# Softmax attention of a hybrid decoder step: the row sums inverted as 128 by 2 and spread by a product, one head's turned scores copied by VectorE, a third buffer for mask rows, another queue order

## The chip, the cores and the metric

The kernel runs on one core of one Trainium2 chip. Its engines run side by side and meet through semaphores: TensorE (PE; its weight loads are shown apart as PEld), VectorE (DVE), ScalarE (ACT), GpSimd (POOL) and SyncE (SP), which here only issues transfers from HBM. The metric is the device time of one execution in microseconds.

## The reference

One inference step of a decoder trunk for 512 prompt tokens and 8 sample tokens (each with 256 past tokens) that share all weights. The first layer has dilated softmax attention (8 heads) beside gated linear attention, the second has sparse attention with an indexer that picks up to 128 keys per query (16 heads, 4 of keys and values). Each layer ends with a feed-forward part. What matters here is the softmax, which both layers share:

```python
def gathered_attention(q, kg, vg, bias, valid):
    ...
    s = jnp.einsum('btngd,btknd->btkng', qg, kg).reshape(bx, t, k, h).astype(jnp.float32) + bias
    s = jnp.where(valid[..., None], s, -jnp.inf)
    lse = jax.nn.logsumexp(s, axis=2)
    p = jnp.exp(s - lse[:, :, None, :]).reshape(bx, t, k, n_kv, grp)
    o = jnp.einsum('btkng,btknd->btngd', p.astype(vg.dtype), vg).reshape(bx, t, h, d)
    return o, lse
```

## The kernel before

The kernel is written engine by engine: each engine has its own program, in the order in which it is written, and waits on semaphores by hand. Most of the span is one long weight stream: SP loads weight blocks of 512 KB into `w_raw` (two places), ScalarE splits off their high part (L1115), GpSimd their low part (L451, `w_lo`), and TensorE multiplies (L567). SP's `weights(b0, b1)` waits before each load until the block of two loads earlier has been split (`w_lo`).

Between the projections stand the two attention stages. Instead of gathering keys, each computes dense causal scores and adds a mask that holds the position bias and what is left out.

- **Stage A** (first layer; 246 to 333.5 us of the span): 4 pairs of heads by 4 blocks of 128 queries, 16 units.
- **Stage C** (second layer; 1005.5 to 1161 us): 8 pairs by 4 blocks, 32 units.

A **unit** is one pair of heads and one block `qb` of queries; its width is W = 128 (qb + 1) keys: 128, 256, 384, 512, and again. The 512 queries of a pair lie in `q_hiC` and `q_loC` (high and low parts, split by GpSimd).

The loop `attention` is written once on each of TensorE, ScalarE and VectorE, and its iteration i works on several units at once:

- **TensorE**: `scores(i)` (L645, three products a head, waits `t_x` until the scores of unit i-1 have been read), `turn(i-1)` (L657, transposes of the exponentials, 128x128 each, in PSUM bank 2 + head; waits `t_e` and, for the bank, `t_c`), `out(i-2)` (L669, weights times values; waits `t_c` and `t_n`). Behind that, without a wait, the **sums product** (L674): the row sums in `stat` spread over 64 columns and multiplied with the identity, so that PSUM holds each query's sum once per output row, 128x128 in the second quarter of bank 4 + u % 2; it counts `t_v`.
- **ScalarE**: `exps(i)` (L1188, one exponential a head, its row sum into `stat`; waits `t_v` of unit i-2, since `stat` has two places, and `t_x`), then `copy(i-1)` (L1198, both heads from PSUM to `tmp` or `ptC`; waits `t_t`, counts `t_c`).
- **VectorE**: `add_bias(i)` (L1481, score plus mask, with the running row minimum into `stat`; waits `t_s`, in stage C also `C_bm`), then `normalise(i-3)`: reciprocal of the 128x128 sums in PSUM (L1490) and product with the unit's output (L1492), counted in `t_n`.
- **GpSimd**, in stage C: splits each pair's queries (L541, L543) and makes each unit's mask, `biasC` plus `score`, the indexer's cut (L551, counts `C_bm`).
- **SP**: `pair_biases` fetches a pair's mask rows from `scratch_rows` into `biasA` or `biasC`, two transfers of 256 KB a pair, one for each head. There are two places, so pair p waits until pair p-2 has been read.

On top of the loop lies the attention of the sample group (`between(i)`): in stage C its score products (`kcC`, L1029, iterations 3 to 6 and 12 to 15, one key cache each) and value products (`vcC`, L1042, iterations 20 to 23 and 27 to 30); its top-k on VectorE is a rank search with one step in each of iterations 2 to 10 (a maximum of eight, L1854, and a replacement). The key caches of sequences 4 to 7 take the places of the first four (`key pages`), and so do the values (`value pages`).

SP's queue ahead of and in stage C, in order: eight weight blocks with the indexer's pages; four weight blocks with key and value pages 0 to 3; six weight blocks; mask rows of pairs 0 and 1; key pages 4 to 7 (each waits until a place is free, `s_ks`); pairs 2 to 5; value pages 4 to 7 (`s_vs`); pairs 6 and 7; the weights after the attention. The indexer's products stand ahead of stage C, so that weight blocks that SP has issued before then wait for them.

## Time and profile before

| | before |
|---|---|
| device time, median of 3 runs | 1668.53 us (1666.94 to 1675.33) |
| the profiled execution | 1665.83 us, of which the span is 1664.0 us |
| PE busy | 1540.6 us (93%) |
| DVE busy | 726.3 us (44%) |
| ACT busy | 631.8 us (38%) |
| POOL busy | 653.2 us (39%) |
| mean granted TensorE clock | 0.95 |
| HBM | 139.11 MB read, 6.76 MB written |

### The profile page before, as it was taken

Reading aid. Unit: us, or ns where it says so; the run is one execution under the profiler, and the core shown is the slowest. Engines: PE = TensorE matmul, PEld = TensorE weight load, DVE = VectorE, ACT = ScalarE, POOL = GpSimd, SP = SyncE. Lnnn points to the kernel's source line nnn. Section 1 sums busy time; section 2 is a strip of 40 time slices with the busy share of each in tenths; the row PEclk is TensorE's granted clock in tenths of the full one; section 3 lists DMA queues with packets and bytes.
Section 4 is the critical chain, followed back from the end, with each engine's and each line's share of the span. In section 5 each row is a group of like instructions: output and inputs, shape, how many; then the busy total and the mean of one; then the engine's idle time right before and its main releaser. Section 6 shows DMA issues by size and latency. Waiting matters only on the chain.

```text
span 1664.0 us, 31509 instructions
## 1 busy us (share of the span) xinstructions
PE 1540.6 (93%) x12374; PEld 1451.0 (87%) x12374; DVE 726.3 (44%) x1119; ACT 631.8 (38%) x1050; POOL 653.2 (39%) x310
## 2 busy tenths in 40 slices
PE   3999989999999999999888997767999999999998
PEld 2999976799999999999887685545999999999998
DVE  5034225555545442213422766545555455422133
ACT  3242356434344333223533344334343433332224
POOL 2432250034444444443443145423344444444434
PEclk9999889899999999999988797788999999999999
DMA  3231143213223223332224022111223222333323
GB/s 128 87 107 64 63 177 103 83 63 102 88 92 97 88 88 102 101 98 92 66 93 134 26 67 70 41 44 39 76 90 97 92 88 88 90 99 101 100 82 123
DMA packets 53986, 146.88 MB, mean 88 GB/s; under 512 B 5485, under 2 KB 19593, under 8 KB 53402
## 3 DMA queue, kind: packets, MB, share of 16 engines
q1 hardware_dynamic: 52538, 139.27, 26.6%
q10 hardware_dynamic: 1376, 6.62, 1.1%
q8 instruction: 48, 0.79, 0.2%
q14 instruction: 24, 0.20, 0.0%
HBM read 139.11 MB, written 6.76 MB: 88 GB/s over the span
## 4 chain that ended last, share of the span: by engine, by line
PE 75%; issue 12%; DVE 4%; ACT 4%; POOL 3%; DMA 2%; SPq 1%; DVEq 0%; POOLq 0%; ACTq 0%
PE PS L567 63%; POOL w_lo L451 2%; DMA biasC<-scratch_rows 2%; PE PS L669 1%; PE PS L657 1%; PE PS L983 1%; PE PS L599 1%; PE PS L645 1%; PE PS L899 1%; PE PS L805 1%; PE PS L806 1%; DVE sqsum L1438 0%; DMA orow<-in_onehots 0%; ACT xC L1188 0%; DVE tmp L1564 0%
## 5 line engine op out<-in xcount | busy, mean ns | idle before, releaser
L451 POOL TENSOR_TENSOR w_lo<-w_raw,w_hi 128x1024 fp32r<-128x1024 f32 x217 | 533.2, 2458 | 868.2 <-ACT w_hi L1115 868.2
L1115 ACT ACTIVATE w_hi<-w_raw 128x1024 fp32r<-128x1024 f32 x217 | 229.8, 1060 | 764.8 <-PE PS L567 758.6
L567 PE MATMUL PS<-act,w_hi 128*128 128x260 f32 x2400 | 498.5, 289 | 20.9 <-POOL act L485 13.5
L567 PE MATMUL PS<-xg_hi,w_hi 128*128 128x260 f32 x1664 | 466.0, 283 | 4.0 <-POOL w_lo L451 4.0
L567 PE MATMUL PS<-xg_lo,w_hi 128*128 128x260 f32 x1664 | 465.4, 283 | 0.0
L567 PE MATMUL PS<-xg_hi,w_lo 128*128 128x260 f32 x1664 | 465.1, 283 | 0.0
L567 PEld LDWEIGHTS PS<-act,w_hi 128*128 128x128 f32 x2400 | 395.7, 194 | 30.6 <-issue 24.5
L567 PEld LDWEIGHTS PS<-xg_hi,w_hi 128*128 128x128 f32 x1664 | 311.6, 189 | 4.4 <-POOL w_lo L451 4.4
L567 PEld LDWEIGHTS PS<-xg_hi,w_lo 128*128 128x128 f32 x1664 | 311.9, 189 | 0.0
L567 PEld LDWEIGHTS PS<-xg_lo,w_hi 128*128 128x128 f32 x1664 | 311.9, 189 | 0.1
L567 PE MATMUL PS<-act,w_lo 128*128 128x260 f32 x944 | 267.9, 288 | 0.0
L567 PE MATMUL PS<-h_hi,w_lo 128*128 128x260 f32 x704 | 198.5, 282 | 0.0
L567 PE MATMUL PS<-h_hi,w_hi 128*128 128x260 f32 x704 | 198.3, 282 | 0.0
L567 PEld LDWEIGHTS PS<-act,w_lo 128*128 128x128 f32 x944 | 182.1, 195 | 0.0
L567 PEld LDWEIGHTS PS<-h_hi,w_hi 128*128 128x128 f32 x704 | 132.5, 188 | 0.0
L567 PEld LDWEIGHTS PS<-h_hi,w_lo 128*128 128x128 f32 x704 | 132.3, 188 | 0.0
L1550 DVE TENSOR_TENSOR x<-PS,x 128x520 f32 x16 | 11.2, 699 | 179.3 <-PE PS L567 179.3
L1538 DVE TENSOR_TENSOR act<-rs,h_hi 128x520 f32 x32 | 72.7, 2273 | 34.8 <-ACT h_hi L1238 34.8
L1532 DVE TENSOR_TENSOR tmp<-tmp,sq 128x520 f32<-128x520 f32 x44 | 59.9, 1361 | 64.2 <-ACT sq L1108 64.1
L1467 DVE SCALAR_TENSOR_TENSOR xg_lo<-x,vecs,xg_hi x32 | 71.9, 2246 | 34.8 <-ACT xg_hi L1140 34.8
L1188 ACT ACTIVATE xC<-xC,statC 128x128 f32<-128x128 f32 (+3 forms) x64 | 35.4, 554 | 87.0 <-PE PS L674 49.9
L1527 DVE TENSOR_TENSOR tmp<-PS,rs 128x520 f32<-128x520 f32 x44 | 30.8, 699 | 76.2 <-PE PS L567 75.2
(313 smaller groups left out, 1816.1 us busy)
## 6 DMA issues: line engine op xcount, KB each, us to landing
w_raw<-in_w SPq DMA_DIRECT2D x217, 512.0 KB, 3.5
biasC<-scratch_rows SPq DMA_DIRECT2D x16, 256.0 KB
yA<-in_cache_k SPq DMA_DIRECT2D x5, 512.0 KB, 6.3
x<-in_xT SPq DMA_DIRECT2D x4, 520.0 KB, 4.9
out_y<-x SPq DMA_DIRECT2D x8, 260.0 KB, 4.3
biasA<-scratch_rows SPq DMA_DIRECT2D x8, 256.0 KB
kcC<-in_pool_k SPq DMA_DIRECT2D x16, 128.0 KB, 2.5
vcC<-in_pool_v SPq DMA_DIRECT2D x16, 128.0 KB, 2.1
```

The source lines that it names most:

```text
L451: pool.tensor_tensor(w_lo[:, s, :], w_raw[:, s, :], w_hi[:, s, :].bitcast(F32), ALU.subtract).then_inc(S("w_lo"), 1)
L567: return pe.matmul(PS[:, 2 * place + half, 0:HALF], w[:, s, j * P:(j + 1) * P], r[:, c, HALF * half:HALF * half + HALF], start=first and n ...
L599: mm = pe.matmul(PS[:, bank + half, 0:HALF], weights, t[:, HALF * half:HALF * half + HALF], start=True, stop=True)
L645: mm = pe.matmul(PS[:, par, 0:W], q_of(pair, ql)[rows, qb * P:(qb + 1) * P], k_of(pair, kl)[rows, 0:W], start=n == 0, stop=n == 2)
L657: mm = pe.transpose(PS[:, 2 + par, cols], xs[:, u % 2, par, cols], ident)
L669: pe.matmul(PS[rows, bank, 0:P], v_of(pair, kb, par), pts[u % 2][:, par, kb * P:(kb + 1) * P], start=kb == 0, stop=kb == qb)
L1115: act.activation(w_hi[:, s, :], w_raw[:, s, :], ACT.Copy).then_inc(S("w_hi"), 1)
L1188: act.activation(xs[:, u % 2, par, 0:W], xs[:, u % 2, par, 0:W], ACT.Exp, bias=stat[:, u % 2, par, 0:1], scale=-1.0, accum_out=stat[:, u % ...
L1467: dve.scalar_tensor_tensor(xg_lo[:, one, :], x[:, one, :], vecs[:, bass.ds(m + gain, 1)], xg_hi[:, one, :].bitcast(F32), ALU.mult, ALU.sub ...
L1527: dve.tensor_tensor(halves(tmp[:, 0, :]), slot(0), halves(rs[:, 0, :]), ALU.mult).then_inc(S("free_v"), 1)
L1532: dve.tensor_tensor(tmp[:, 1, :], tmp[:, 1, :], sq[:, 0, :], ALU.mult).then_inc(S("f_s"), 1)
L1538: dve.tensor_tensor(lo, rs[:, 1:2, :], h_hi[:, bass.ds(f, 1), :].bitcast(F32), ALU.subtract).then_inc(S("h_lo"), 1)
```

## The change

**Loop.** The row sums are inverted where they stand, as 128 by 2 (`invert(i-1)` on VectorE), and it is the inverse that TensorE spreads by the same product. ScalarE copies the spread 128x128 from PSUM to `rr` (`spread(i-2)`), and VectorE's `normalise(i-3)` is only the product. The turned scores of the first head are copied by ScalarE (`t_c`), those of the second by VectorE (`t_d`). `stat` has four places instead of two, and the exponentials wait for the small reciprocal (`t_r`) of four units back. ScalarE's order is copy(i-1), exps(i), spread(i-2).

**Mask rows.** Stage C has three places: the two of `biasC`, and a part of `yC` that holds the indexer's queries before (free after `i_r` 24 and `d_z` 3). Stage A keeps two. In SP's queue pairs 0 and 1 stand ahead of the six weight blocks; then pairs 2 and 3, key pages 4 to 7, pairs 4 to 7, value pages 4 to 7.

**Names.** Semaphores of both stages are put together under common names (`smp_*`, `split_hi`, `split_lo`, `v_turned`, `v_ok`), with counts that go on.

```diff
...
-        statC = sb("statC", [P, 2, 2, 4], scope=sC)
+        statC = sb("statC", [P, 4, 2, 4], scope=sC)
...
+        biasC_place = (biasC[:, 0], biasC[:, 1], yC[:, 2:4, 0:SEQ])
...
-            def pair_biases(pairs, dst, rows, read, each):
+            def pair_biases(pairs, place, depth, rows, read, each):
...
-                    if p >= 2:
-                        sp.wait_ge(S(read), each * QB * (p - 1))
+                    if p >= depth:
+                        sp.wait_ge(S(read), each * QB * (p - depth + 1))
...
-                        sp.dma_start(dst[:, p % 2, par, :], src).then_inc(S(f"bias{p % 2}"), 16)
+                        sp.dma_start(place[p % depth][:, par, :], src).then_inc(S(f"bias{p % depth}"), 16)
...
+            def biases_c(*pairs):
+                pair_biases(pairs, biasC_place, 3, rows_c, "C_bm", 1)
+
             for b in range(4):
                 weights(B_C + 2 + NS + b, B_C + 3 + NS + b)
                 key_pages(b)
                 value_pages(b)
+            biases_c(0, 1)
             weights(B_C + 2 + NS + 4, B_OUT1 + 2)
-            rows_c = lambda p, par: 8 + 4 * (2 * (p // 4) + par) + p % 4
-            pair_biases(range(2), biasC, rows_c, "C_bm", 1)
+            sp.wait_ge(S("i_r"), 24)
+            sp.wait_ge(S("d_z"), 3)
+            biases_c(2, 3)
             for b in range(4, NS):
                 sp.wait_ge(S("s_ks"), NS + b - 3)
                 key_pages(b)
-            pair_biases(range(2, 6), biasC, rows_c, "C_bm", 1)
+            biases_c(4, 5, 6, 7)
             for b in range(4, NS):
                 sp.wait_ge(S("s_vs"), NS + b - 3)
                 value_pages(b)
-            pair_biases(range(6, 8), biasC, rows_c, "C_bm", 1)
...
-                            pe.wait_ge(S("t_c"), 2 * (first + u) + par - 1)
+                            pe.wait_ge(S("t_d" if par else "t_c"), first + u)
...
-                    pe.wait_ge(S("t_c"), 2 * (first + u + 1))
+                    pe.wait_ge(S("t_c"), first + u + 1)
+                    pe.wait_ge(S("t_d"), first + u + 1)
...
+                    pe.wait_ge(S("t_r"), first + u + 1)
                     for par in range(2):
-                        sums = stat[:, u % 2, par, 1:2].to_broadcast([P, HD])
-                        mm = pe.matmul(PS[HD * par:HD * par + HD, bank, P:2 * P], sums, ident,
+                        inverse = stat[:, u % 4, par, 2:3].to_broadcast([P, HD])
+                        mm = pe.matmul(PS[HD * par:HD * par + HD, bank, P:2 * P], inverse, ident,
                                        start=True, stop=True)
...
-                    if first + u > 1:
-                        act.wait_ge(S("t_v"), first + u - 1)
+                    if first + u > 3:
+                        act.wait_ge(S("t_r"), first + u - 3)
...
+                def spread(u):
+                    act.wait_ge(S("t_v"), first + u + 1)
+                    if first + u > 1:
+                        act.wait_ge(S("t_n"), first + u - 1)
+                    act.activation(rr[:, u % 2, :], PS[:, 4 + u % 2, P:2 * P], ACT.Copy).then_inc(S("t_rc"), 1)
...
+                    if 1 <= i <= count:
+                        copy(i - 1)
                     if i < count:
                         exps(i)
-                    if 1 <= i <= count:
-                        copy(i - 1)
+                    if 2 <= i < count + 2:
+                        spread(i - 2)
...
+                def copy(u):
+                    W = unit(u)[2]
+                    if first + u > 1:
+                        dve.wait_ge(S("t_v"), first + u - 1)
+                    dve.wait_ge(S("t_t"), 2 * (first + u) + 2)
+                    dve.tensor_copy(pts[u % 2][:, 1, 0:W], PS[:, 3, 0:W]).then_inc(S("t_d"), 1)
+
+                def invert(u):
+                    dve.wait_ge(S("t_e"), 2 * (first + u + 1))
+                    dve.reciprocal(stat[:, u % 4, :, 2:3], stat[:, u % 4, :, 1:2]).then_inc(S("t_r"), 1)
+
                 def normalise(u):
                     pair, qb, W = unit(u)
-                    bank = 4 + u % 2
-                    dve.wait_ge(S("t_v"), first + u + 1)
-                    if first + u > 1:
-                        dve.wait_ge(S("t_n"), first + u - 1)
-                    dve.reciprocal(rr[:, u % 2, :], PS[:, bank, P:2 * P]).then_inc(S("t_r"), 1)
-                    dve.wait_ge(S("t_r"), first + u + 1)
-                    dve.tensor_tensor(oraw[:, KC + pair, qb * P:(qb + 1) * P], PS[:, bank, 0:P],
+                    dve.wait_ge(S("t_rc"), first + u + 1)
+                    dve.tensor_tensor(oraw[:, KC + pair, qb * P:(qb + 1) * P], PS[:, 4 + u % 2, 0:P],
                                       rr[:, u % 2, :], ALU.mult).then_inc(S("t_n"), 1)
...
                     if i < count:
                         add_bias(i)
+                    if 1 <= i <= count:
+                        copy(i - 1)
+                        invert(i - 1)
                     if 3 <= i < count + 3:
                         normalise(i - 3)
...
```

What this does to the order of work stands best in three places.

ScalarE, inside stage C, two iterations (units 256 and 384 wide), before; `xC` holds the scores, and out<-in stands behind the line of the kernel, with the semaphores that the row waits on:

```order
L1188 ACTIVATE xC,statC<-xC,statC 128x256 [waits t_x,t_v]
L1188 ACTIVATE xC,statC<-xC,statC 128x256 [waits t_x]
L1198 ACTIVATE tmp<-PS 128x128 [waits t_t,t_v]
L1198 ACTIVATE tmp<-PS 128x128 [waits t_t]
L1188 ACTIVATE xC,statC<-xC,statC 128x384 [waits t_x,t_v]
L1188 ACTIVATE xC,statC<-xC,statC 128x384 [waits t_x]
L1198 ACTIVATE ptC<-PS 128x256 [waits t_t,t_v]
L1198 ACTIVATE ptC<-PS 128x256 [waits t_t]
L1202 ACTIVATE act<-oraw 128x512 [waits t_n]
```

The same stretch after the change:

```order
L1206 ACTIVATE tmp<-PS 128x128 [waits t_t,t_v]
L1197 ACTIVATE xC,statC<-xC,statC 128x256 [waits t_x,t_r]
L1197 ACTIVATE xC,statC<-xC,statC 128x256 [waits t_x]
L1212 ACTIVATE workC<-PS 128x128 [waits t_n,t_v]
L1206 ACTIVATE ptC<-PS 128x256 [waits t_t,t_v]
L1197 ACTIVATE xC,statC<-xC,statC 128x384 [waits t_x,t_r]
L1197 ACTIVATE xC,statC<-xC,statC 128x384 [waits t_x]
L1212 ACTIVATE workC<-PS 128x128 [waits t_n,t_v]
L1216 ACTIVATE act<-oraw 128x512 [waits t_n]
```

The copy of the unit before now stands ahead of the exponentials, only the first head's is left, and each iteration ends with the copy of the spread inverse (`workC` is where `rr` lies in stage C).

VectorE, one iteration of stage C, before (`ISA` is the sum of score and mask with its row minimum; the second `ISA` row moves that minimum into `statC`):

```order
L1481 ISA xC,statC<-PS,rs 128x256 [waits t_s,C_bm,t_t]
L1481 ISA statC 128x1
L1481 ISA xC,statC<-PS,rs 128x256 [waits t_s]
L1481 ISA statC 128x1
L1490 RECIPROCAL workC<-PS 128x128 [waits t_n,t_v]
L1492 TENSOR_TENSOR oraw<-PS,workC 128x128 [waits t_r]
```

and after:

```order
L1497 ISA xC,statC<-PS,rs 128x256 [waits t_s,C_bm,t_t]
L1497 ISA statC 128x1
L1497 ISA xC,statC<-PS,rs 128x256 [waits t_s]
L1497 ISA statC 128x1
L1505 COPY tmp<-PS 128x128 [waits t_t,t_v]
L1509 RECIPROCAL statC<-statC 128x2 [waits t_e]
L1514 TENSOR_TENSOR oraw<-PS,workC 128x128 [waits t_rc]
```

The copy of the second head and the small reciprocal stand between the mask sums and the product of the unit three back; the 128x128 reciprocal is gone.

SP's queue from the last value pages of sequence 3 to the first key page of sequence 4 (the branch rows are the loop over weight blocks; `TENSOR_LOAD ptab` reads a page's number), before:

```order
L420 DMA vcC<-in_pool_v 128x256
L331 UNCONDITIONAL_BRANCH
L331 ISA
L328 ISA [waits w_lo]
L328 DMA w_raw<-in_w 128x1024
...
L331 REGISTER_ALU
L331 COMPARE_AND_BRANCH
L348 DMA biasC<-scratch_rows 128x1x512 x4
L404 TENSOR_LOAD ptab [waits s_ks]
```

and after:

```order
L421 DMA vcC<-in_pool_v 128x256
L349 DMA biasC<-scratch_rows 128x1x512 x4
L332 UNCONDITIONAL_BRANCH
...
L329 ISA [waits w_lo]
L329 DMA w_raw<-in_w 128x1024
...
L349 DMA yC<-scratch_rows 128x1x512 [waits d_z,i_r]
L349 DMA yC<-scratch_rows 128x1x512
L349 DMA biasC<-scratch_rows 128x1x512 [waits C_bm]
L349 DMA biasC<-scratch_rows 128x1x512
L405 TENSOR_LOAD ptab [waits s_ks]
```

Pairs 0 and 1 (four transfers, `x4`) moved from behind the six weight blocks to ahead of them, and pairs 2 and 3 now stand between the blocks and the key pages, pair 2 with a wait for the third place.

## Rows read from the trace of the kernel before

**Rows 1.** Stages: stretch, length, busy (x) PE to POOL, clock, DMA share, GB/s.
```profile
246.00:333.50 87.50, 81.59 (x626) 60.08 (x626) 49.80 (x132) 43.09 (x124) 6.66 (x7) 0.89 0.32 99
1005.50:1161.00 155.50, 111.91 (x910) 83.78 (x910) 90.53 (x263) 64.39 (x204) 60.53 (x45) 0.81 0.13 43
1050.00:1055.00 5.00, 4.58 (x29) 3.31 (x30) 4.17 (x15) 1.96 (x8) 3.99 (x3) 0.50 0.13 50
1085.00:1090.00 5.00, 4.01 (x34) 2.67 (x34) 3.81 (x9) 3.75 (x13) 2.99 (x4) 1.00 0.02 5
```

**Rows 2.** Chain that ended last: start, us, what; two longest waits.
```profile
1034.42 12.88 DMA biasC<-scratch_rows
...
1111.32 12.87 DMA biasC<-scratch_rows
```

**Rows 3.** TensorE's timeline: start, us, line, out<-in [idle before <-what ended it].
```profile
1033.60 0.43 PE L645 MATMUL PS<-act,q_hiC 64*128 64x128 f32 x2
...
1048.66 0.81 PE L645 MATMUL PS<-act,q_hiC 64*128 64x256 f32 x3 [9.37 <-DVE statC L1481]
...
1108.44 0.45 PE L645 MATMUL PS<-k_C,q_hiC 64*128 64x128 f32 x4
...
1125.55 0.81 PE L645 MATMUL PS<-k_C,q_hiC 64*128 64x256 f32 x3 [13.27 <-DVE statC L1481]
...
1132.94 0.79 PE L645 MATMUL PS<-k_C,q_hiC 64*128 64x512 f32 x4
```

**Rows 4.** TensorE's timeline between those two waits.
```profile
1068.40 0.52 PE L645 MATMUL PS<-act,q_hiC 64*128 64x256 f32 x4
...
1077.12 1.14 PE L1029 MATMUL PS<-kcC,qzC 128*128 128x257 f32 x4
...
1078.19 0.45 PE L645 MATMUL PS<-k_C,q_hiC 64*128 64x128 f32 x4
...
1079.28 1.06 PE L657 MATMUL PS<-const,xC 128*128 128x128 f32 x8 [0.53 <-ACT tmp L1198]
...
1081.30 0.51 PE L645 MATMUL PS<-k_C,q_hiC 64*128 64x256 f32 x4
```

**Rows 5.** Waits of 1005 to 1161: engine, tile, line <- releaser: us, times, longest.
```profile
ACT xC L1188 <- PE PS L674: 49.9, 27, 4.0
```

**Rows 6.** TensorE's groups by shape, 1005.5 to 1161: busy, mean ns | idle before.
```profile
L657 PE MATMUL PS<-const,xC 128*128 128x128 f32 x160 | 30.0, 321 | 11.4 <-ACT tmp L1198 7.8 <-ACT ptC L1198 3.6
```

**Rows 7.** GpSimd's timeline, first mask sum of pair 3.
```profile
1057.92 0.73 POOL L551 TENSOR_TENSOR sq<-biasC,score 128x256 f32<-128x256 f32 x1 [1.64 <-DMA biasC<-scratch_rows]
```

**Rows 8.** SP's issues, 905 to 960.
```profile
909.46 1.44 SPq L420 DMA_DIRECT2D vcC<-in_pool_v  x2
944.59 14.65 SPq L328 DMA_DIRECT2D w_raw<-in_w  x3
```

**Rows 9.** DMA issues, 1110 to 1125: times, KB, median us from issue to landing.
```profile
w_raw<-in_w SPq DMA_DIRECT2D x1, 512.0 KB, 15.7
```

**Rows 10.** DMA issues of the whole span (page, part 6).
```profile
w_raw<-in_w SPq DMA_DIRECT2D x217, 512.0 KB, 3.5
```

**Rows 11.** ScalarE's groups by line and shape, 1004 to 1160.
```profile
L1198 ACT ACTIVATE tmp<-PS 128x128 f32<-128x128 f32 x16 | 3.4, 258 | 0.0
```

**Rows 12.** VectorE's groups by line and shape, 1004 to 1160.
```profile
L1490 DVE RECIPROCAL workC<-PS 128x128 f32<-128x128 f32 x32 | 30.5, 952 | 1.2 <-PE PS L674 1.2
...
L1854 DVE MAX8 mx<-wk 8x8 f32<-8x257 f32 x7 | 2.8, 406 | 0.0
...
L1832 DVE COPY vtokC<-PS 128x512 f32<-128x512 f32 x2 | 1.3, 676 | 0.0
...
L1587 DVE RECIPROCAL sstC<-sstC 128x1 f32<-128x1 f32 x1 | 0.2, 152 | 0.0
```

**Rows 13.** TensorE's weight loads, timeline, 1021 to 1024.
```profile
1022.43 0.63 PEld L669 LDWEIGHTS PS<-tmp,vtokC 128*64 128x64 f32 x12 [0.17 <-issue]
1023.03 0.25 PEld L674 LDWEIGHTS PS<-const,statC 128*64 128x64 f32 x4
```

More of the change, by code:

```diff
@@ L550, in _ @@
                 mask = score[:, qb, 0:W].unsqueeze(1).to_broadcast([P, 2, W])
-                pool.tensor_tensor(bmC[u % 2][:, :, 0:W], biasC[:, pair % 2, :, SEQ - W:SEQ], mask,
+                pool.tensor_tensor(bmC[u % 2][:, :, 0:W], biasC_place[pair % 3][:, :, SEQ - W:SEQ], mask,
                                    ALU.add).then_inc(S("C_bm"), 1)
@@ L882, in _ @@
             mm.then_inc(S("s_o"), 1)
-            pe.wait_ge(S("A_v"), QB)
+            pe.wait_ge(S("v_ok"), QB)
             pe.wait_ge(S("b_o"), 1)
             def ready_a(pair):
-                pe.wait_ge(S("A_st"), (1, 2, 5, 6)[pair])
+                pe.wait_ge(S("split_lo"), (1, 2, 5, 6)[pair])
                 pe.wait_ge(S("k_split"), 1)
@@ L1009, in _ @@
                 if kb % 2:
-                    mm.then_inc(S("C_vt"), 1)
+                    mm.then_inc(S("v_turned"), 1)
             sample_index(8)
-            pe.wait_ge(S("C_vtc"), 2)
+            pe.wait_ge(S("v_ok"), 6)
             def ready_c(pair):
-                pe.wait_ge(S("C_st"), pair + 1)
+                pe.wait_ge(S("split_lo"), 6 + pair + 1)
                 pe.wait_ge(S("k_split"), 3)
@@ L1178, in products_in, with attention @@
                     head_rms(q, q % 2)
-            def attention(first, count, xs, pts, stat, between):
+            def attention(first, count, xs, pts, stat, rr, between):
                 def exps(u):
                     W = unit(u)[2]
-                    if first + u > 1:
-                        act.wait_ge(S("t_v"), first + u - 1)
+                    if first + u > 3:
+                        act.wait_ge(S("t_r"), first + u - 3)
                     for par in range(2):
@@ L1195, in copy @@
                         act.wait_ge(S("t_v"), first + u - 1)
-                    for par in range(2):
-                        act.wait_ge(S("t_t"), 2 * (first + u) + par + 1)
-                        act.activation(pts[u % 2][:, par, 0:W], PS[:, 2 + par, 0:W], ACT.Copy).then_inc(S("t_c"), 1)
+                    act.wait_ge(S("t_t"), 2 * (first + u) + 1)
+                    act.activation(pts[u % 2][:, 0, 0:W], PS[:, 2, 0:W], ACT.Copy).then_inc(S("t_c"), 1)
+                def spread(u):
[3 more added lines that the diff above has]
+                    act.activation(rr[:, u % 2, :], PS[:, 4 + u % 2, P:2 * P], ACT.Copy).then_inc(S("t_rc"), 1)
                 def high_out(pair):
@@ L1469, in gained_lo, with attention @@
                                          ALU.subtract).then_inc(S("xg_lo"), 1)
-            def attention(first, count, xs, stat, rr, bias, between):
+            def attention(first, count, xs, pts, stat, rr, bias, between):
                 def add_bias(u):
@@ L1710, in _ @@
                 dst = qz[rows, 32 * r:32 * r + 31 * 65 + 1:65].rearrange("p (t b) -> p t b", t=4)
[L1711 removed]
+                dve.tensor_copy(dst, yA[rows, Y_Q:Y_Q + 4, SEQ:NT]).then_inc(S("smp_q"), 1)
             def new_key_a(b):
```

146 lines of the change are left out of this document (73 added, 73 removed).

## The prediction

> **What bounds the kernel now.** I read the busy shares first (table above): TensorE is busy 93% of the span, so time comes off only where TensorE stands still or runs at its lower clock. The view by stages shows where: in stage A it is busy 81.59 of 87.50 us at a mean granted clock of 0.89, in stage C 111.91 of 155.50 us at 0.81 [rows 1]. Everything that the diff touches lies in these two stages. The chain that ended last then shows two waits on a transfer of mask rows in stage C, 12.88 us at 1034.42 and 12.87 us at 1111.32 [rows 2]; no other transfer of that length stands on it there. TensorE's own timeline gives the price: scores of iteration 8 start at 1033.60 and those of iteration 9 at 1048.66; iteration 24 starts at 1108.44 and iteration 25 at 1125.55 [rows 3]. After each stall the clock is down (0.50 in 1050 to 1055, against 1.00 in 1085 to 1090 [rows 1]).
>
> The measure for an undisturbed iteration is 1068.40 to 1081.30: four iterations (scores 256, 384, 512 and 128 wide) take 12.90 us, three of them with a product for the sample group, 1.07 us from its start to the next product's [rows 4]. Less these 3.2 us that is 9.7 us for four, 2.4 us each, and only 0.53 us of it is a wait for ScalarE. So where sample products fill the gaps TensorE is nearly the bound already. The loop that the diff rewires (ScalarE's exponentials wait for the sums product of two units back: 49.9 us of ScalarE idle [rows 5]) costs TensorE far less than that idle time suggests: all waits before the turning products in stage C are 11.4 us [rows 6].
>
> **The change, part by part.**
>
> Third buffer and queue order. With two buffers the rows of pair p may be fetched only once pair p-2 has been read, one pair ahead, which at the pace above is 9.7 us. The transfer takes 12.9 us [rows 2], or 10.6 us when the next follows on its heels: pair 2 landed at 1034.42 + 12.88 = 1047.30, pair 3 released GpSimd at 1057.92 after a wait [rows 7]. 9.7 is less than 10.6, so two buffers are late even with prompt issue, and these two were not issued promptly: pair 2 stood on SP behind the key pages, pair 6 behind the value pages. Three buffers give two pairs of lead, 19.4 us, against 12.9; and pairs 2 and 6 now stand ahead of the pages that held them. I take both stalls as gone: 15.06 - 2.58 = 12.5 us and 17.11 - 2.58 = 14.5 us, where 2.58 is the iteration of the same shape, 1078.19 to 1081.30 less its wait of 0.53 [rows 3, 4]. **-27.0 us.**
>
> The slow clock behind the stalls goes with them. From 1048.66 to 1068.40 four iterations with one sample product took 19.74 us, 18.7 without it, against 9.7; I take 8.5 of these 9.0 because there is a second, small sample product in it. From 1125.55 to 1132.94 two took 7.4 against 4.9 [rows 3, 4]. **-11.0 us.** Lower bound 0, if TensorE finds no other work to keep its clock.
>
> What moves past what: pairs 0 and 1 now go out right after the value pages issued at 909.46, ahead of six weight loads, of which the first goes out at 944.59 [rows 8]. A weight load that stood behind mask rows took 15.7 us to land [rows 9], others 3.5 [rows 10]. Four transfers at 10.6 us a pair are through by about 911 + 21 = 932, so the indexer's products, which hold the next load back until 944.59, cover them with 12 us to spare; without that cover the first load would be up to 21 us late. Cost 0.
>
> ScalarE's and VectorE's part of the loop. Exponentials of unit u no longer wait for the sums product of u-2, and the copies of the two turned heads run on two engines at once. ScalarE gives up one copy per unit (258 ns or more) and gets the spreading copy of 128x128 from PSUM, for which the same-sized row gives 258 ns [rows 11]: nothing or less. VectorE loses the 128x128 reciprocal, 952 ns, and gets a reciprocal of 128x2 (152 ns for 128x1; at most the old 952) and a copy of one head, at most 676 ns for 512 columns [rows 12]. By the nearest rows that is -0.12 us at the widest unit; if the small reciprocal cost as much as the big one, +0.68. I take the first, as time per instruction here follows the columns. What this frees on TensorE is bounded by 0 and the 11.4 us of rows 6; part of those lie in the stretches already counted, and the start and the end keep theirs: **-6 us**. In stage A, where TensorE idles 5.9 us [rows 1], I take **-3**, between 0 and 5.9: its sample products cover half the stage already.
>
> Costs. VectorE carries one step of the sample group's rank search in each of nine iterations; its maximum alone takes 406 ns [rows 12], and the step has a second instruction over the same 257 columns, so some 0.9 us by estimate. Four of these iterations have a sample product on TensorE beside them, the other five do not, so VectorE could set the pace there: 0 to 4.5 us, I take **+2.3**. TensorE gets a new wait (for the small reciprocal) in the middle of what ran without a break: weight loads behind a wait show 0.17 us of issue time, those of the sums product, which had none, show nothing [rows 13]. 48 units by 0.17 is 8.2 us at most, and where TensorE waits anyway it costs nothing: **+6**. Behind a waiting sums product stand the next scores; the reciprocal that it waits for is issued an iteration earlier, so the wait itself should be empty.
>
> GpSimd's mask sums, renamed semaphores and the four-deep statistics change no work: 0.
>
> **Sum.** -27.0 - 11.0 - 6 - 3 + 2.3 + 6 = -38.7 us. On the profiled execution's own 1665.83 us that is 1627.1. The median of the runs stands 2.7 above it (1668.53), so I predict **1630 us**.
>
> **Rivals.**
>
> (1) A second bound takes the loop's place. VectorE (90.53 us busy in stage C [rows 1]) now holds a copy that waits for TensorE between the mask sum of one unit and that of the next, and ScalarE's copy stands ahead of the exponentials. If that in-order coupling costs what the old one cost, nothing of the 6 and 3 us comes, and the costs come in full (4.5 + 8.2): -27 - 11 + 12.7 = -25.3, 1643 us. For it: VectorE is the busier of the two. Against: every engine's sum per unit falls. Chance 0.16.
>
> (2) Mask rows or pages late again. If one of the two stalls stays (pair 6 or 7, because the faster loop asks sooner), 17 us of the gain are lost: 1647 us. For it: a pair's transfer (10.6 to 12.9 us) is no shorter than the new pace of a pair. Against: the 19.4 us of lead. The value pages 4 to 7 now go out behind pair 7; they are issued after iteration 20 and used in 27, seven iterations or about 17 us, against the 12.9 us that the rows ahead of them can last. Chance 0.08 for both. The Trainium skill, DMA: Bandwidth & Descriptors, section "Queues, rings and completion order", says that each DMA engine takes one queue's descriptors in ring order; by that rule those pages, which share SP's queue, wait for pair 7's rows, and would cost up to 12.9 us if the lead were used up. The trace agrees: 15.7 us for the load behind mask rows [rows 9], 3.5 for others [rows 10].
>
> (3) Slower than before: the clock. The new loop puts more, shorter waits between TensorE's products. Were the granted clock to stay at 0.50 (1.2 GHz) through stage C, eight rounds of 18.7 us and 16 sample products at twice 1.07 us would make 184 us, against 155.5 now: 1697 us. It decides from about two thirds of the stage's work on: at full clock the same work is 8 x 9.7 + 17 = 95 us, and (155.5 - 95) / (184 - 95) = 0.68. Against: in 1085 to 1090 the clock is 1.00 with TensorE busy 4.01 of 5 us [rows 1]. Chance 0.03.
>
> (4) Everything goes, the costs are nothing: -27 - 11 - 11.4 - 5.9 = -55.3, 1613 us. Chance 0.05.
>
> **How the numbers follow.** My forecast has 0.68. The range reaches from (4) to (2), 1612 to 1647, and leaves out (3) and a little on either side. A measurement of this kernel tells about 0.5% (8 us) from no change; only (3), and both stalls staying, fall outside "faster": faster 0.94, same 0.03, slower 0.03.
>
> **What would show it.** Right: no mask transfer on the chain within stage C; TensorE's scores start without a gap of more than 4 us after iteration 4; granted clock of stage C above 0.9; stage C some 115 to 120 us from first scores to the output projection instead of 155.5; stage A 84 to 87 us. The first weight load after the indexer lands in about 3.5 us. Wrong: a wait of GpSimd on mask rows (then rival 2), VectorE without idle time in stage C and TensorE waiting for its copies or row sums (rival 1), a clock under 0.8 there (rival 3). The step I trust least is the cost of the added wait on TensorE, which no row shows at that place.

## The result and the profile after

The changed kernel takes 1625.6 us (median of 4, 1623.1 to 1631.1) beside 1671.7 us for the kernel before, a ratio of 0.973 with an interval of 0.970 to 0.976. Timed once more beside the last experiments it took 1631.0 us (1619.4 to 1637.6), 0.977 of before (0.973 to 0.981). The forecast was 1630 us in 1612 to 1647.

| | after |
|---|---|
| the profiled execution | 1623.13 us, of which the span is 1621.3 us |
| PE busy | 1531.9 us (94%) |
| DVE / ACT / POOL busy | 708.2 / 628.8 / 652.4 us |
| mean granted TensorE clock | 0.961 |

Nearly all of the difference lies in stage C. The view by stages, with the columns of [rows 1], from the first score product of each attention stage to the first product of the output projection:

```profile
1004.74:1121.10 116.36, 103.22 (x910) 77.80 (x911) 80.55 (x294) 62.77 (x204) 60.81 (x45) 0.91 0.16 51
244.16:330.76 86.60, 84.20 (x627) 63.03 (x627) 42.13 (x148) 41.83 (x124) 6.54 (x7) 0.85 0.32 100
```

Stage C is now 116.4 us at a clock of 0.91; before it ran from 1005.57 to 1161.28, 155.7 us, at 0.81. Stage A is 86.6 us; before it ran from 246.10 to 333.54, 87.4 us. The spans differ by 42.7 us: 39.4 from stage C, 0.8 from stage A, and 2.5 from the rest of the execution.

TensorE's timeline, where the two stalls stood in [rows 3]: first scores of the stage, scores of iterations 8, 9, 24, 25 and 31.

```profile
1004.74 0.69 PE L652 MATMUL PS<-act,q_hiC 64*128 64x128 f32 x4 [1.47 <-DVE vtokC L1857]
...
1034.13 0.54 PE L652 MATMUL PS<-act,q_hiC 64*128 64x128 f32 x4
...
1037.58 0.61 PE L652 MATMUL PS<-act,q_hiC 64*128 64x256 f32 x3 [0.67 <-DVE statC L1497]
...
1089.09 0.44 PE L652 MATMUL PS<-k_C,q_hiC 64*128 64x128 f32 x4
...
1092.21 0.52 PE L652 MATMUL PS<-k_C,q_hiC 64*128 64x256 f32 x4
...
1109.64 0.74 PE L652 MATMUL PS<-k_C,q_hiC 64*128 64x512 f32 x4
```

Iterations 8 and 24 take 3.45 and 3.12 us, where they took 15.06 and 17.11. From first to last scores the stage takes 1109.64 - 1004.74 = 104.9 us, and 142.4 before (1005.57 to 1148.00). That stretch is the measure of the experiments below, since the rest of an execution disturbs it less than it does the time. The granted clock in the stage's first iterations still differs from execution to execution (table of experiment 9).

The groups by line and shape of stage C show the loop's terms (busy us, mean ns of one, idle before and what ended it): the turning products and the spreading product on TensorE, the copy and the small reciprocal on VectorE, ScalarE's spreading copy.

```profile
L664 PE MATMUL PS<-const,xC 128*128 128x128 f32 x160 | 27.1, 303 | 0.4 <-ACT xC L1197 0.3
...
L683 PE MATMUL PS<-const,statC 128*64 128x128 f32 x128 | 13.1, 285 | 0.0
...
L1505 DVE COPY ptC<-PS 128x512 f32<-128x512 f32 x8 | 5.5, 689 | 2.9 <-PE PS L664 2.9
...
L1509 DVE RECIPROCAL statC<-statC 128x2 f32<-128x2 f32 x32 | 5.0, 157 | 0.0
...
L1212 ACT ACTIVATE workC<-PS 128x128 f32<-128x128 f32 x32 | 8.4, 261 | 3.9 <-PE PS L683 2.7 <-DVE oraw L1514 1.1
```

The turning products waited 11.4 us in [rows 6] and wait 0.4 now; the spreading product, which has the new wait, never stood idle ahead. The single prices are as read: 157 ns for the small reciprocal, 689 for a copy of 512 columns, 261 for the spreading copy.

### The profile page after: what moved, and what is told of

Same layout as the page of the kernel before. It is cut to its first block, busy times and chain, and to the rows that moved or that the text cites. A ratio compares the mean times of both kernels' runs of the same rounds, so it can differ in the third digit from the quotient of the medians.

```text
span 1621.3 us, 31604 instructions
## 1 busy us (share of the span) xinstructions
PE 1531.9 (94%) x12374; PEld 1446.1 (89%) x12374; DVE 708.2 (44%) x1167; ACT 628.8 (39%) x1050; POOL 652.4 (40%) x310
## 4 chain that ended last, share of the span: by engine, by line
PE 76%; issue 12%; DVE 5%; ACT 3%; POOL 3%; DMA 0%; SPq 0%; DVEq 0%; POOLq 0%; ACTq 0%
PE PS L574 65%; POOL w_lo L458 2%; PE PS L652 2%; PE PS L992 1%; PE PS L606 1%; PE PS L664 1%; PE PS L677 1%; PE PS L908 1%; PE PS L1038 1%; DVE sqsum L1454 0%; PE PS L814 0%; PE PS L815 0%; DMA orow<-in_onehots 0%; DVE tmp L1589 0%; ACT tmp L1115 0%
## 5 line engine op out<-in xcount | busy, mean ns | idle before, releaser
L574 PE MATMUL PS<-act,w_hi 128*128 128x260 f32 x2400 | 497.8, 289 | 19.3 <-POOL act L492 12.7
L1575 DVE TENSOR_TENSOR x<-PS,x 128x520 f32 x16 | 11.2, 700 | 179.3 <-PE PS L574 179.3
L1552 DVE TENSOR_TENSOR tmp<-PS,rs 128x520 f32<-128x520 f32 x44 | 30.8, 700 | 75.8 <-PE PS L574 75.1
L1561 DVE TENSOR_TENSOR rs<-PS,tmp 128x520 f32<-128x520 f32 x44 | 30.8, 700 | 59.1 <-PE PS L574 58.9
```

The lines of the kernel that those rows point to most:

```text
L574: return pe.matmul(PS[:, 2 * place + half, 0:HALF], w[:, s, j * P:(j + 1) * P], r[:, c, HALF * half:HALF * half + HALF], start=first and n ...
L1552: dve.tensor_tensor(halves(tmp[:, 0, :]), slot(0), halves(rs[:, 0, :]), ALU.mult).then_inc(S("free_v"), 1)
L1561: dve.tensor_tensor(halves(rs[:, 1, :]), slot(1), halves(tmp[:, 1, :]), ALU.mult).then_inc(S("free_v"), 1)
```

## The experiments

The theory that the forecast rests on: the late mask rows carry the gain, by third place and queue order together, and the loop gives and costs about the same. The rivals: one of third place and order does it alone; or the loop carries a part of its own, by VectorE's reciprocal, by the two copies, or by ScalarE's order.

**1. The rows alone.** The loop of before, with three places and the new queue order:

```diff
-            pair_biases(range(2), biasC, rows_c, "C_bm", 1)
...
+            biases_c(0, 1)
             weights(B_C + 2 + NS + 4, B_OUT1 + 2)
+            sp.wait_ge(S("i_r"), 24)
+            sp.wait_ge(S("d_z"), 3)
+            biases_c(2, 3)
```

> The loop of before, with the third place and the new queue order alone. Theory (the mask rows carry the gain: both stalls and the slow clock behind them): about 36 of the 42 us come, time 1634 us (1629 to 1640) where before is 1671, stage C 118 to 122 us from its first scores to the output projection, no scores later than 4 us after iteration 8 or 24. Rival (the old loop, in which ScalarE's exponentials wait for the sums product, is the next bound as soon as the stalls are gone): 1645 us or more, iterations at 3.2 us or longer in the middle of the stage.

Measured: 1643.5 us, 0.982 of before (0.977 to 0.987); 112.2 us from first to last scores (1013.95 to 1126.12), 30.3 less than before. No scores came late by a stall (iteration 8 took 5.65 us, 24 took 3.76), but 7.3 us are left to the changed kernel. The profiled executions differ by more, spans of 1643.6 and 1621.3 us: 10.6 in stage C up to the output projection, 6.9 in stage A. ScalarE's wait from 1030 us on, in the columns of [rows 5]:

```profile
ACT xC L1195 <- PE PS L681: 45.4, 27, 4.0
```

And the turning products' group, first to last scores, in the columns of [rows 6]:

```profile
L664 PE MATMUL PS<-const,xC 128*128 128x128 f32 x146 | 25.2, 300 | 12.5 <-ACT tmp L1205 6.8 <-ACT ptC L1205 5.7
```

ScalarE's wait for the sums product is nearly as long as in [rows 5], and what TensorE pays for it as in [rows 6], 12.5 us. Both expectations are half right: the rows carry most, and the old loop is the next bound. The time lies between the two ranges (up to 1640, from 1645).

**2. The loop alone.** After the change, with two places and the old queue order:

```diff
-                pair_biases(pairs, biasC_place, 3, rows_c, "C_bm", 1)
+                pair_biases(pairs, biasC_place, 2, rows_c, "C_bm", 1)
...
-            biases_c(0, 1)
             weights(B_C + 2 + NS + 4, B_OUT1 + 2)
+            biases_c(0, 1)
...
-            biases_c(4, 5, 6, 7)
+            biases_c(2, 3, 4, 5)
...
+            biases_c(6, 7)
```

> The loop after the change, with two places and the queue order of before. Theory (the stalls are set by when the transfer is issued and how long it takes, not by the loop): both stalls stay, a little longer since the loop asks earlier; the gain is that of stage A and of the iterations between the stalls, 2 to 6 us: 1665 to 1669 us where before is 1671. Rival (the loop carries half of the gain): 1650 us or less.

Measured: 1653.9 us, 0.990 of before (0.988 to 0.992), 17 us faster, outside of what the theory allowed and short of the rival's 1650. In its profile the stalls stand as before (iterations 8 and 24 take 14.89 and 17.81 us), and first to last scores take 133.9 us (1016.89 to 1150.77), 8.5 less than before. With the 30.3 of the rows alone that makes 38.8, and both together gave 37.5: the two parts add up, and the loop is worth about 8 us in this stage, not nothing. The profile is of the slowest of five executions (1664.0 us); where the other ones are 7 to 14 us shorter was not seen.

**3 and 4. Which of place and order.** After the change, three places in the old order (experiment 3):

```diff
-            biases_c(0, 1)
             weights(B_C + 2 + NS + 4, B_OUT1 + 2)
+            biases_c(0, 1)
```

Two places in the new order (experiment 4):

```diff
-        biasC_place = (biasC[:, 0], biasC[:, 1], yC[:, 2:4, 0:SEQ])
+        biasC_place = (biasC[:, 0], biasC[:, 1])
...
-                pair_biases(pairs, biasC_place, 3, rows_c, "C_bm", 1)
+                pair_biases(pairs, biasC_place, 2, rows_c, "C_bm", 1)
```

> After the change, three places kept, the queue order of before. Theory (pairs 2 and 6 are late because they stand behind pages that wait for iterations 3 to 6 and 20 to 23): both stalls stay, 8 to 14 us each with the slow clock behind them, 1650 to 1664 us. Rival (the third place is what removes the stalls, the order does nothing): 1624 to 1630 us.

> After the change, the new queue order with two places (a pair may be fetched when the pair two back has been read). Theory (one pair's lead, 9.7 us at the full pace, is less than the 10.6 to 12.9 us of a transfer, so pairs are late even in the best order): pairs 2 to 7 late by 1 to 4 us each, 8 to 20 us in all, 1634 to 1646 us. Rival (the order alone removes the stalls, the third place does nothing): 1624 to 1629 us.

Three places in the old order: 1659.3 us, 0.993 of before (0.991 to 0.995), in the theory's range, and the stalls as they were. TensorE's scores of iterations 24 and 25:

```profile
1098.82 0.45 PE L652 MATMUL PS<-k_C,q_hiC 64*128 64x128 f32 x4
...
1116.08 0.81 PE L652 MATMUL PS<-k_C,q_hiC 64*128 64x256 f32 x3 [14.08 <-DVE statC L1497]
```

Two places in the new order: 1635.5 us, 0.978 of before (0.976 to 0.980), which by itself lies within the theory's range. The trace decides against it. GpSimd's waits in stage C:

```profile
POOL rs L556 <- DVE statC L1495: 27.6, 14, 5.0
POOL sq L556 <- DVE statC L1495: 18.8, 10, 5.4
POOL sq L556 <- DMA biasC<-scratch_rows: 0.2, 1, 0.2
```

Its last mask sum of pair 1 and its first of pair 3, on its timeline:

```profile
1056.68 2.37 POOL L556 TENSOR_TENSOR rs<-biasC,score 128x1024 f32<-128x1024 f32 x1 [0.95 <-DVE statC L1495]
...
1073.83 0.74 POOL L556 TENSOR_TENSOR sq<-biasC,score 128x256 f32<-128x256 f32 x1 [0.22 <-DMA biasC<-scratch_rows]
```

All mask rows together cost one wait of 0.2 us. Iterations 8 to 18 and 24 to 30 take within 0.04 us each what they take after the change. What is longer in this execution lies elsewhere: stage C begins at 1018.65, after a stretch at a lower clock (last section), iterations 3 and 4 take 12.7 us against 10.5, and 20 and 21, behind the wait of a sample product, 11.1 against 8.3. So the order alone removes the stalls, and the third place is not needed at this pace, though with two places the rows of pair 3 come with nothing to spare (the wait of 0.22 us).

**5 and 6. Parts of the loop.** Both heads copied by ScalarE (experiment 5):

```diff
-                    act.wait_ge(S("t_t"), 2 * (first + u) + 1)
-                    act.activation(pts[u % 2][:, 0, 0:W], PS[:, 2, 0:W], ACT.Copy).then_inc(S("t_c"), 1)
+                    for par in range(2):
+                        act.wait_ge(S("t_t"), 2 * (first + u) + par + 1)
+                        act.activation(pts[u % 2][:, par, 0:W], PS[:, 2 + par, 0:W], ACT.Copy).then_inc(S("t_c"), 1)
```

The sums spread, with the 128x128 reciprocal on VectorE, which keeps its copy (experiment 6):

```diff
-                        inverse = stat[:, u % 4, par, 2:3].to_broadcast([P, HD])
+                        inverse = stat[:, u % 4, par, 1:2].to_broadcast([P, HD])
...
+                    dve.reciprocal(rr[:, u % 2, :], PS[:, 4 + u % 2, P:2 * P]).then_inc(S("t_rc"), 1)
```

> After the change, with both turned heads copied by ScalarE again; inverse, four-deep statistics and ScalarE's order kept. Theory (what held the old loop back is VectorE, with its 128x128 reciprocal in every iteration): little is lost, 0 to 4 us; stage C 105 to 109 us from first to last scores (104.9 after the change). Rival (the copies in a row on ScalarE held it back): most of the loop's 7 to 8 us in stage C is lost, 111 us or more.

> After the change, with the sums spread as before and the 128x128 reciprocal from PSUM on VectorE in place of the 128x2 one and ScalarE's spreading copy; VectorE keeps the copy of one head. Theory (VectorE's reciprocal): VectorE has 0.95 us more an iteration, some 26 us in the stage, with the copy on top; all of the loop's gain goes and more, 112 to 122 us from first to last scores, 1633 to 1645 us. Rival (the copies): 105 to 107 us, 1625 to 1629 us.

Copies on ScalarE: 1624.1 us, 0.975 of before (0.970 to 0.980), no change. First to last scores 108.5 us (1000.16 to 1108.68), of which 2.9 us come from iterations 20 and 21 (11.2 against 8.3); iterations 5 to 18 take what they took, within 0.2 us each. Splitting the copies gives nothing.

Sums spread: 1657.4 us over nine executions (1637.3 to 1660.8), 0.991 of before (0.988 to 0.994); its profile, of the fastest of them, shows 108.6 us (1013.29 to 1121.88) from first to last scores. A second time it took 1645.6 us (1639.5 to 1657.4), 0.988 of before, with 111.7 us (1012.23 to 1123.94):

> The same kernel as the one with the sums spread, for a second profile: its profiled execution took 1637 us and the median of its nine 1657. Theory (the same waits let the granted clock stay low in more or less of stages A and C, so that executions differ): a profile near the median shows a lower clock in one of these stages, and the rest alike. Rival (the lost time lies in the weight streams outside of the stages): stages A and C as in the first profile, the rest longer.

Its loop in stage A takes 66.2 us in both profiles (first to last scores), 61.9 after the change. VectorE is what differs in stage C, in the columns of [rows 1]:

```profile
1013.29:1121.88 108.59, 98.25 (x842) 74.00 (x842) 91.95 (x268) 52.88 (x163) 60.71 (x45) 0.91 0.17 55
```

92.0 us of 108.6, against 74.0 of 104.9 after the change: with the copy and the big reciprocal it carries both. Neither expectation of the first run holds: 108.6 us lies between their ranges, and the time is longer than both allow. The two profiles are both of executions near 1640 us, so where the slower ones lose more than these 8 to 11 us was not seen and stays open. The record of every execution shows only that it goes with TensorE's clock: a mean granted clock of 0.954 and 0.955 in the four of up to 1643 us, 0.941 to 0.948 in the nine from 1648 to 1661 us. Neither expectation of the second run is decided.

**7 and 8. A shorter transfer.** Mask rows kept eight times in `scratch_rows` instead of twice, so that a transfer has eight pieces of 16 partitions; in the kernel before (experiment 7) and after the change (experiment 8):

```diff
-                        src = bass.AP(tensor=a["rows"].tensor, offset=2 * h * RW + P - 1,
-                                      ap=[[RW - P // 2, 2], [-1, P // 2], [1, SEQ]])
+                        src = bass.AP(tensor=a["rows"].tensor, offset=8 * h * RW + P - 1,
+                                      ap=[[RW - P // 8, 8], [-1, P // 8], [1, SEQ]])
```

> The kernel before, with the mask rows written eight times instead of twice so that a transfer has eight pieces of 16 partitions instead of two of 64; two places and the old queue order kept. Theory (the transfer is long because it uses two of the 16 DMA engines, its DMA share is 0.13): a pair lands in about a quarter of 12.9 us, 3 to 4 us, each of the two stalls falls by about 9 us and the slow clock behind them by half: 1642 to 1652 us. Rival (bytes or small rows in HBM set the length): no change, 1668 to 1673 us.

> After the change, with the same eight pieces. Theory (mask rows are off the path after the change): nothing, 1622 to 1629 us, stage C within 1 us of 104.9 from first to last scores. Rival (late mask rows still set the pace of GpSimd's masks somewhere): 4 us or more faster.

In the kernel before: 1657.6 us, 0.993 of before (0.990 to 0.996); iterations 8 and 24 take 7.17 and 9.77 us, 7.9 and 7.3 less, and first to last scores 126.7 us (1014.36 to 1141.10). The view by stages while rows are in flight:

```profile
1112.00:1114.00 2.00, 0.27 (x3) 0.13 (x2) 0.00 (x0) 0.00 (x0) 0.00 (x0) 1.00 0.43 120
```

The two waits of GpSimd that are left, on its timeline:

```profile
1050.72 0.72 POOL L551 TENSOR_TENSOR sq<-biasC,score 128x256 f32<-128x256 f32 x1 [8.87 <-DMA biasC<-scratch_rows]
...
1116.91 0.72 POOL L551 TENSOR_TENSOR sq<-biasC,score 128x256 f32<-128x256 f32 x1 [12.14 <-DMA biasC<-scratch_rows]
```

The DMA share is 0.43, where it was 0.13 in [rows 1]. The Trainium skill, DMA: Bandwidth & Descriptors, section "Why a DMA increments its semaphore by 16 and not by 1", says that a transfer issued by SP uses the largest number of engines, at most 16, that divides the slowest dimension on both sides; two pieces then use 2 of 16 and eight use 8. The trace agrees in size: shares of 0.13 and 0.43 beside 2/16 and 8/16. A faster transfer halves the stalls and doesn't remove them, since the rows still stand behind the pages. On SP's timeline they are issued at 1045.02 and 1110.74, right behind the pages:

```profile
1032.33 12.64 SPq L415 DMA_DIRECT2D kcC<-in_pool_k  x8
1045.02 29.06 SPq L348 DMA_DIRECT2D biasC<-scratch_rows  x8
1099.75 10.95 SPq L420 DMA_DIRECT2D vcC<-in_pool_v  x8
1110.74 3.37 SPq L348 DMA_DIRECT2D biasC<-scratch_rows  x4
```

GpSimd had by then waited for 3.2 and 6.0 us; the other 5.7 and 6.2 us of its waits are the transfer of the pair, where the expectation had 3 to 4. The stalls fell by 7.9 and 7.3 us instead of 9, and the time misses the expected 1642 to 1652. After the change it gives nothing: 1628.0 us, 0.974 of before (0.969 to 0.978), 104.9 us from first to last scores.

**9. Only ScalarE's order and depth.** Both parts of the loop undone together, as in experiments 5 and 6: sums spread, big reciprocal, both copies on ScalarE. What differs from experiment 1, beside the semaphores' names, is ScalarE's order (copy ahead of the exponentials), the four places of `stat`, and with them the wait; against experiment 1:

```diff
-                    if first + u > 1:
-                        act.wait_ge(S("t_v"), first + u - 1)
+                    if first + u > 3:
+                        act.wait_ge(S("t_v"), first + u - 3)
...
+                    if 1 <= i <= count:
+                        copy(i - 1)
                     if i < count:
                         exps(i)
-                    if 1 <= i <= count:
-                        copy(i - 1)
```

> After the change, with the sums spread and the 128x128 reciprocal on VectorE as before and both turned heads copied by ScalarE as before; of the loop's change only ScalarE's order (copy ahead of the exponentials) and the four-deep statistics stay, so that the exponentials wait for the product of four units back. Theory (the big reciprocal itself, on VectorE's way between two mask sums, is what held the loop): as with the sums spread and the copies on two engines, 108 to 112 us in stage C from first to last scores, stage A's loop 65 us or more, well above the changed kernel in time. Rival (order and depth on ScalarE are the gain, and the small reciprocal only pays for VectorE's copy): 104 to 107 us, stage A's loop 61 to 63 us, 1623 to 1630 us.

> The changed kernel itself, on the same chip as the others of this call, as their measure: 1622 to 1630 us, 0.970 to 0.976 of before.

Measured: 1631.1 us (1629.6 to 1637.2), 0.978 of before (0.975 to 0.980), beside 1631.0 us for the changed kernel. First to last scores 101.0 us (1013.34 to 1114.29), less than after the change (104.9, and 107.3 the second time, 1005.71 to 1113.05); stage A's loop 63.5 us. The turning products' group of this stretch:

```profile
L664 PE MATMUL PS<-const,xC 128*128 128x128 f32 x146 | 23.5, 291 | 0.0
```

Against experiment 1 the 12.5 us of waits are gone, with the same big reciprocal on the same engine. The theory that VectorE's reciprocal held the loop falls, and the rival's cause stands, though none of its three ranges was met exactly (101.0 us where it had 104 to 107, stage A's loop 63.5 where it had 61 to 63, 1631.1 where it had up to 1630).

Part of these lengths goes with the granted clock, in no order that the edits explain: in iteration 3, and in iteration 20 behind the wait for a sample copy, the longer times stand at the lower clock. The last column leaves out the first five iterations, and 20 and 21:

| | iteration 3, us | clock | iteration 20, us | clock | iterations 5 to 30 less 20 and 21, us |
|---|---|---|---|---|---|
| rows alone (1) | 5.0 | 1.00 | 5.1 | 0.67 | 86.1 |
| order and depth (9) | 4.7 | 1.00 | 3.5 | 1.00 | 77.2 |
| after | 6.9 | 0.60 | 5.1 | 0.67 | 75.9 |
| after, second time | 7.3 | 0.61 | 5.1 | 0.66 | 75.9 |
| copies on ScalarE (5) | 8.2 | 0.50 | 6.4 | 0.50 | 75.8 |
| sums spread (6) | 6.3 | 0.73 | 5.1 | 0.66 | 80.0 |

By the last column the loop gives 10.2 us in stage C, and ScalarE's order and depth are 8.9 of them (some of it by the clock too: iteration 8 runs at 0.72 in experiment 1 and at 1.00 here, and takes 5.6 and 3.7 us). The first five iterations go the other way, 17.4 us in experiment 1, 17.1 here and 20.7 after the change, by VectorE's copy (next section) and by the clock. In stage C the small reciprocal and the spreading copy for the most part only pay for VectorE's copy, which gives nothing (experiments 5 and 6). In stage A order and depth are half of it: 65.2 us in experiment 1, 63.5 here, 61.9 after the change. Order and depth were not parted.

**10. What was left.** After the change, with the placing of the sample queries moved ahead of the stage, where VectorE waits, and the sample product of iteration 19 moved to iteration 20:

```diff
-                if i in (0, 1):
-                    place_queries(i)
...
+            for t in range(NS):
+                dve.wait_ge(S("hn_ok"), 14 + t)
...
+                    ins = dve.tensor_copy(cols[:, c0:c0 + 7 * 129 + 1:129], yC[rows, 10 + t, SEQ:NT])
...
-                if i == 19:
+                if i == 20:
                     pe.wait_ge(S("smp_diag"), 2)
```

> After the change, with VectorE's placing of the sample queries (2.44 and 4.41 us inside iterations 0 and 1) moved to where VectorE stands idle before the stage, and the sample product that waits 1.9 us in iteration 19 moved to iteration 20. Theory (what is left in stage C is VectorE at its start and that one wait with the lower clock behind each): 5 to 9 us less in stage C, 96 to 100 us from first to last scores, 1616 to 1621 us. Rival (the start is bound by ScalarE, GpSimd or TensorE at its lower clock): 0 to 2 us.

Measured: 1613.7 us (1609.3 to 1619.4), 0.967 of before (0.965 to 0.970), beside 1631.0 us and 0.977 (0.973 to 0.981) for the changed kernel: faster, also than the theory's 1616 to 1621. First to last scores 96.1 us (1002.09 to 1098.22), at a clock of 0.96:

```profile
1002.09:1098.22 96.13, 93.07 (x843) 70.02 (x843) 67.33 (x255) 57.44 (x191) 60.80 (x45) 0.96 0.19 62
```

The first four iterations take 11.8 us instead of 17.1, and iterations 19 and 20 take 6.9 instead of 10.4. Not all of the gain is the edit's. The span is 13.8 us shorter than in the first profile of the changed kernel and 17.2 than in the second; 8.8 and 11.2 of that lie from first to last scores, but 3.1 and 6.0 in stage A, which the edit doesn't touch (83.55 us here at a clock of 0.89, 86.60 and 89.50 there at 0.85 and 0.82).

## Why the prediction was right

The total came out and the stalls went as forecast. The third place, on which half of the argument stood, was not needed, and two terms missed in opposite directions.

**The stalls (-27.0 us).** They went, 25.6 us of them (15.06 - 3.45 and 17.11 - 3.12); 22.8 of these came with the rows alone, the rest with the loop. But the step "9.7 is less than 10.6, so two buffers are late even with prompt issue" failed. 9.7 us is a pair's pace less its sample products, yet the products take their time too: with them four iterations took 12.90 us [rows 4]. Experiment 4 shows it: pair 1's last mask sum ends at 1056.68 + 2.37 = 1059.05 and pair 3's first starts at 1073.83, 14.8 us later, more than the 12.9 us of a transfer. Of the two reasons given, the place in the queue was the whole of it (experiments 3 and 4).

**The slow clock behind them (-11.0 us).** Iterations 9 to 12 and 25 to 26 gave 5.8 and 3.3 us, together 9.2, of which 6.0 came with the rows alone. This clock was the stalls' doing, as forecast: in experiment 3, where the stalls are back, iteration 9 takes 4.12 us at a granted clock of 0.50, against 2.66 at 1.00 after the change.

**The loop in stage C (-6 + 2.3 + 6 = +2.3 us).** Here sizes were off. From the rows alone to the full change stage C loses 7.3 us more. The waits before the turning products went from 12.5 to 0.4 us: nearly the whole bound of [rows 6], of which the forecast took half. The added wait on TensorE, +6, cost nothing: the spreading product's idle time is 0.0. The +2.3 for the rank search was no cost of the change in four of the five iterations that it named: 7 to 10 take 14.4 us with the old loop and no stall, 11.9 after the change. In the fifth, iteration 2, a cost of 1.3 us came, by another cause: VectorE's new copy stands between the mask sums while VectorE also places the sample queries. Iteration 2 takes 5.5 to 5.6 us in the kernels that have that copy and 4.2 in those that don't (before, experiments 1, 5, 7 and 9); with the placing moved it takes 3.57 (experiment 10). Iteration 3 takes 4.7 to 8.2 us over all kernels: 8.2 at a granted clock of 0.50 (experiments 2 to 5 and 7), 6.3 to 7.3 at 0.60 to 0.73, 4.7 to 5.0 at 0.83 to 1.00 (experiments 1, 9 and 10). Why the clock rises earlier in some was not tried.

The rows alone were forecast at -38 us and gave -30.3, the loop at +2.3 and gave -7.3. The two misses nearly cancel, so that the sum came out closer than its terms is in part luck.

**Stage A (-3 us).** Its loop got 3.8 us shorter (65.7 to 61.9, first to last scores), but stage A as a whole only 0.8. The rest was given back at the end. Stage A's last stretch after the change, and the same work before:

```profile
318.00:322.00 4.00, 4.00 (x40) 3.81 (x40) 1.18 (x4) 1.21 (x3) 0.00 (x0) 0.83 0.00 0
322.00:326.00 4.00, 4.00 (x21) 4.00 (x20) 0.60 (x1) 0.00 (x0) 0.00 (x0) 0.50 0.02 4
326.00:330.00 4.00, 3.18 (x15) 3.05 (x14) 0.60 (x3) 0.08 (x1) 0.00 (x0) 0.50 0.00 0
```

```profile
320.00:324.00 4.00, 4.00 (x33) 3.50 (x31) 0.81 (x1) 1.72 (x3) 0.00 (x0) 0.66 0.00 0
324.00:328.00 4.00, 4.00 (x47) 3.81 (x46) 2.29 (x5) 0.38 (x1) 0.00 (x0) 1.00 0.00 0
328.00:332.00 4.00, 3.97 (x26) 3.85 (x25) 0.69 (x1) 0.25 (x1) 0.00 (x0) 0.69 0.02 4
```

The same 16 sample products take 3.45 us there at the lower clock and 1.95 before at the full one:

```profile
320.50 3.45 PE L919 MATMUL PS<-ptsA,vcA 128*128 128x2 f32 x16
```

```profile
326.19 1.95 PE L910 MATMUL PS<-ptsA,vcA 128*128 128x2 f32 x16
```

What the loop gained in this execution the lower clock behind it took back; why it fell there was not tried. In the second profile of the changed kernel the loop takes 61.5 us and the stage 89.5, longer than before, and over all kernels the stage takes 82.9 to 95.6 us. So the loop's part of the -3 came, and a gain of the whole stage is not shown.

**Rivals.** Little of the second bound (1) came: VectorE's copy cost 1.3 us in iteration 2, not the 12.7 of that rival. No pages or rows came late (2): GpSimd waits for no transfer in stage C. The clock (3) went the other way, 0.91. Of (4), the costs at nothing and nearly all of the 11.4 us in stage C came true; stage A's 5.9 did not. Of the signs named ahead, one failed: scores still start more than 4 us apart in iterations 12 (4.8 us), 19 (5.2) and 20 (5.1); the last two are the wait and the clock of experiment 10.

## What to carry to other kernels

When a transfer is late, read first what stands ahead of it in its queue, and only then count buffers: the pace against which a buffer's lead is measured must hold all the work of the loop, side work too. An engine's idle time in a loop is worth what the bounding engine waits for it (12 us of TensorE here, of 45 us on ScalarE), and the cheapest way to get it can be another order and a deeper buffer, with no arithmetic moved. A term that sums several edits should be tested edit by edit, since errors of opposite sign hide in a right total.

## What was not expected of the hardware

**The clock differs in stretches that the change does not touch.** In 925 to 950 us, the indexer ahead of stage C, the changed kernel and the one with two places in the new order, in the columns of [rows 1]:

```profile
925.00:950.00 25.00, 24.60 (x132) 18.12 (x133) 21.09 (x54) 9.54 (x17) 4.78 (x3) 0.80 0.12 42
```

```profile
925.00:950.00 25.00, 23.22 (x55) 11.69 (x54) 14.70 (x26) 8.51 (x18) 0.00 (x0) 0.50 0.13 45
```

The instructions up to there are the same on TensorE; stage C begins at 1004.74 and at 1018.65. Two profiles of the changed kernel agree (1004.74 and 1005.71), and two of the one with the sums spread (1013.29 and 1012.23). Why kernels differ there stays open. Over all kernels stage C begins at 1000 to 1019 us, so a difference of that size between two times above is not by itself an edit's; the stage's own stretch decides.

**Small copies on VectorE beside GpSimd.** Ten copies of 64x8 take 1.85 us in experiment 10, while GpSimd stands idle; eight take 2.44 and 4.41 us after the change, while GpSimd makes mask sums and splits queries:

```profile
982.41 1.85 DVE L1856 COPY qzC<-yC 64x8 f32<-64x8 f32 x10
```

```profile
1006.39 2.44 DVE L1869 COPY qzC<-yC 64x8 f32<-64x8 f32 x8
...
1009.83 4.41 DVE L1869 COPY qzC<-yC 64x8 f32<-64x8 f32 x8
```

**A wait of 1.9 us can cost more than itself.** After the change TensorE waits 1.89 us for a sample copy in iteration 19; in the columns of [rows 1], the 5 us of that wait, the 5 us after it and the next:

```profile
1071.00:1076.00 5.00, 3.11 (x30) 2.45 (x29) 3.48 (x13) 2.50 (x8) 1.41 (x2) 0.90 0.13 47
1076.00:1081.00 5.00, 5.00 (x46) 4.09 (x46) 1.68 (x7) 1.93 (x8) 1.67 (x1) 0.76 0.14 50
1081.00:1086.00 5.00, 5.00 (x54) 4.16 (x50) 2.34 (x12) 3.19 (x12) 4.60 (x4) 1.00 0.31 98
```

The clock is 0.76 behind the wait. Iterations 19 to 21 take 13.5 us after the change and 10.0 in experiment 10, where the wait is gone: 3.5 us for a wait of 1.9. It isn't always so. Behind the same wait of 1.9 us the clock in iteration 20 is 1.00 in experiments 2 and 3, and the three iterations take 11.9 us, the wait and no more; in experiments 4 and 5 it is 0.50, and they take 16.5. What decides between these was not tried.
